# Feed-forward norms whose inverse root arrives behind the products, and a last expert turn without a gather

## The reference

```python
# first block, at its end
x = x + moe(rmsnorm(x, g_ffn), ...)               # top 4 of 32 experts, 3 x 1024x1024 weights each
gate = sigmoid(rmsnorm(x, g_ple) @ w_ple_gate)    # 1024x1024
x = x + (p @ w_ple_proj) * gate
x = rmsnorm(x, g_final)
# each of the two layers
x = x + 0.5 * swiglu(rms_norm(x, ffa_norm), ffa_w_in, ffa_w_out)   # 1024 -> 2 x 2816 -> 1024
h = rms_norm(x, mix_norm); ...                    # three mixers, gated and summed
x = x + (sum of gated branches) @ w_out
x = x + 0.5 * swiglu(rms_norm(x, ffb_norm), ffb_w_in, ffb_w_out)

def rms_norm(x, g): return x * rsqrt(mean(x * x, -1) + 1e-6) * g
def swiglu(h, w_in, w_out): gate, up = split(h @ w_in); return (silu(gate) * up) @ w_out
```

## Time and profile before

| | us |
|---|---|
| median of 3 runs | 2454.72 |
| lowest, highest | 2454.32, 2455.74 |
| profiled execution | 2455.39 |
| its span | 2453.6 |
| PE busy | 2419.6 |
| POOL busy | 1013.1 |
| DVE busy | 920.0 |
| ACT busy | 888.6 |

### The profile page before, as it was taken

One profiled execution on the slowest core, in us unless ns is written; L12 is line 12 of the kernel. 1 busy time (PEld: TensorE's weight loads), 2 busy tenths in 40 slices (PEclk: granted clock), 3 DMA queues, 4 the chain that ended last, 5 costly groups with the idle time before them and its releaser, 6 DMA issues.

```text
span 2453.6 us, 34874 instructions
## 1 busy us (share of the span) xinstructions
PE 2419.6 (99%) x13863; PEld 1713.7 (70%) x13863; DVE 920.0 (37%) x1736; ACT 888.6 (36%) x1457; POOL 1013.1 (41%) x430
## 2 busy tenths in 40 slices
PE   8999999999999999999999999999999999999999
PEld 6744444444444444468889899888888898998887
DVE  5622222222222222262248764332432388653322
ACT  6411111101111110154457624544444477425443
POOL 0000000000000000048877436788788785546886
PEclk9999999999999999999999999999999999999999
DMA  8799999999999999935555224465555553334654
GB/s 291 291 427 429 429 430 429 430 430 429 430 429 431 429 430 429 413 102 197 189 164 180 95 96 145 161 203 190 166 198 189 166 184 112 121 100 150 202 186 144
DMA packets 96584, 653.07 MB, mean 266 GB/s; under 512 B 10864, under 2 KB 13336, under 8 KB 69848
## 3 DMA queue, kind: packets, MB, share of 16 engines
q1 hardware_dynamic: 96472, 651.51, 69.1%
HBM read 650.22 MB, written 1.25 MB: 266 GB/s over the span
## 4 chain that ended last, share of the span: by engine, by line
PE 88%; DMA 8%; DVE 2%; ACT 1%; issue 1%; POOL 0%; SPq 0%; DVEq 0%; ACTq 0%
PE bank L2256 22%; PE bank L831 13%; PE bank L631 10%; PE bank L633 10%; PE bank L632 10%; PE bank L832 7%; DMA ring<-in_expert_units 4%; PE bank L2243 4%; DMA scratch<-in_expert_units 4%; PE bank L1226 3%; PE bank L2264 2%; PE bank L2272 1%; PE bank L1104 1%; PE bank L1075 1%; PE bank L1182 0%
## 5 line engine op out<-in xcount | busy, mean ns | idle before, releaser
L618 POOL TENSOR_TENSOR w_lo<-raw,w_hi 128x1024 fp32r<-128x1024 f32 (+2 forms) x424 | 1009.2, 2408 | 1198.2 <-ACT w_hi L612 1198.2
L2256 PE MATMUL bank<-ring,scratch 128*64 128x512 f32 x2304 | 513.4, 596 | 8.6 <-DMA ring<-in_expert_units 8.6
L831 PE MATMUL bank<-hT_both,w_hi 128*128 128x512 f32 x1408 | 498.3, 398 | 1.7 <-DVE hT_both L722 1.7
L612 ACT CAST w_hi<-raw 128x1024 fp32r<-128x1024 f32 (+2 forms) x424 | 422.3, 1042 | 169.1 <-PE bank L633 155.5
L832 PE MATMUL bank<-hT_both,w_lo 128*128 128x256 f32 x1408 | 395.9, 281 | 0.0
L2256 PEld LDWEIGHTS bank<-ring,scratch 128*64 128x64 f32 x2304 | 160.0, 137 | 323.2 <-issue 318.3
L831 PEld LDWEIGHTS bank<-hT_both,w_hi 128*128 128x128 f32 x1408 | 265.1, 188 | 67.6 <-issue 3.4
L2489 DVE TENSOR_TENSOR scratch<-bank,scratch 128x512 f32<-128x512 f32 x64 | 44.3, 692 | 594.8 <-PE bank L2272 590.7
L832 PEld LDWEIGHTS bank<-hT_both,w_lo 128*128 128x128 f32 x1408 | 266.7, 189 | 0.6
L909 DVE TENSOR_REDUCE scratch<-bank 128x256 f32<-128x512 f32 x88 | 60.8, 691 | 358.4 <-PE bank L832 358.4
L2256 PE MATMUL bank<-scratch 128*64 128x512 f32 x768 | 172.1, 596 | 2.2 <-DMA scratch<-in_expert_units 2.1
(11 more groups left out here) (372 smaller groups left out, 3360.1 us busy)
## 6 DMA issues: line engine op xcount, KB each, us to landing
ring<-in_expert_units SPq DMA_DIRECT2D x144, 2048.0 KB, 25.0
raw<-in_layer_halves SPq DMA_DIRECT2D x408, 512.0 KB, 4.4
scratch<-in_expert_units SPq DMA_DIRECT2D x47, 2048.0 KB, 25.9
ring<-in_first_units SPq DMA_DIRECT2D x11, 1024.0 KB, 10.0
ring<-in_ple_units SPq DMA_DIRECT2D x2, 2048.0 KB, 18.6
raw<-in_layer_halves SPq DMA_DIRECT2D x8, 424.0 KB, 3.4
scratch<-in_norm_gains SPq DMA_DIRECT2D x6, 512.0 KB, 6.1
raw<-in_layer_halves SPq DMA_DIRECT2D x4, 384.0 KB, 3.6
```

The lines of the kernel that those rows point to most:

```text
L612: k.nc.scalar.copy(k.w[0][i % SPLIT_SLOTS][:, at], k.raw[n % RAW_SLOTS][:, 0:at.stop - at.start]).then_inc(k.shared("weights_hi"), 1)
L618: k.nc.gpsimd.tensor_tensor(k.w[1][i % SPLIT_SLOTS][:, at], k.raw[n % RAW_SLOTS][:, 0:at.stop - at.start], k.w[0][i % SPLIT_SLOTS][:, at], ...
L831: nc.tensor.matmul(bank[:, :], w[0], both, start=start, stop=False)
L2256: last = nc.tensor.matmul(b[g * SL:(g + 1) * SL, :], lhsT[:, c, :], w[:, c, g, :], start=start and c == 0, stop=stop and c == 3)
```

## The change

Three parts.

1. **The root comes behind the products**, in all four norms ahead of a feed-forward block. DVE writes h = x * gain (`lnorm_gained`) as soon as a quarter of x is done, and PE transposes that. ACT and DVE compute the root meanwhile; DVE multiplies the unit matrix by it (`diag_dve`), PE multiplies ones by the two diagonals (`rstd_pe`), and the bank then holds the root of token s in column s of each partition. DVE copies it (128x256) and multiplies the gate sum and the up sum of each (u, j) by it: two more 128x256 products for each of the 22 column blocks of a block. The order of unit 0 is new (`ffn_first_pe`): half the columns of x first, so that the last quarter is turned behind 4 or 8 pairs, and the root's product stands before the last 8 pairs. The transposes move into the work ahead: into the last gate product, the last w_out product, the last feed-forward product. All spare products go, except four in layer 1's first norm. Squares are written to a scratch place instead of h.
2. **The fold with the final norm**: x is written back to SBUF before it is scaled, so projection banks come free earlier; the gained product and the final gain are two separate products; the final scaling is one 128x1024 step for each t, after the diagonals.
3. **The last turn**: the last group of four turns is written out behind the loop. In the last turn PE does no gather, only counts its semaphore up, and turns the selection before the transposes.

```diff
+def lnorm_gained(k, dve, n, t, half):
+    at = columns_half(half)
+    if t + half == 0:
+        dve.wait_ge(*k.at("gain_loaded", 16 * (n + 1)))
+    k.nc.vector.tensor_tensor(k.h[:, t, at], k.x[:, t, at], k.s(GAIN, D)[:, at], ALU.mult).then_inc(k.sem("h_ready"), 1)
+
+def diag_dve(k, dve, n, scales):
+    for t in range(NT):
+        dve.wait_ge(*k.at("norm_rstd", 4 * n + t + 1))
+        last = k.nc.vector.tensor_scalar(k.s(RSTD_DIAG, NT, P)[:, t, :], k.c("ident"), scales[t], None, ALU.mult)
+    last.then_inc(k.sem("diag_ready"), 1)
+
+def rstd_pe(k, pe, n):
+    b, full = k.claim(pe, ("rstd", n))
+    pe.wait_ge(*k.at("diag_ready", n + 1))
+    for t in range(NT):
+        last = k.nc.tensor.matmul(b[:, t * P:(t + 1) * P], k.c("ones"), k.s(RSTD_DIAG, NT, P)[:, t, :], start=(t == 0), stop=(t == NT - 1))
+    last.then_inc(full, 1)
...
+def late_norm_act(k, act, n, x_ready, between):
...
     square(0, 0)
     square(0, 1)
+    lnorm_hi(k, act, n, 0, 0)
+    lnorm_hi(k, act, n, 0, 1)
     lnorm_hi(k, act, n, 1, 0)
+    between()
+    if n == 2:
+        lnorm_hi(k, act, n, 1, 1)
+    square(1, 0)
+    square(1, 1)
+    if n == 0:
+        lnorm_hi(k, act, n, 1, 1)
+    lnorm_root(k, act, n, 0)
+    lnorm_root(k, act, n, 1)
+
+def late_norm_dve(k, dve, link, n, evacuate, x_written):
+    def gained(t, half):
+        evacuate(t, half)
+        x_written(t, half)
+        lnorm_gained(k, dve, n, t, half)
+    gained(0, 0)
+    gained(0, 1)
+    gained(1, 0)
+    lnorm_lo(k, dve, n, 0, 0)
+    lnorm_lo(k, dve, n, 1, 0)
+    gained(1, 1)
+    lnorm_lo(k, dve, n, 0, 1)
+    lnorm_lo(k, dve, n, 1, 1)
+    for t in range(NT):
+        lnorm_variance(k, dve, link, n, t)
+    diag_dve(k, dve, n // 2, [k.s(STATS, 8)[:, 2 * t:2 * t + 1] for t in range(NT)])
...
+def ffn_first_pe(k, pe, n):
...
+    if n == 0:
+        block(0, 0)
+        last_turned()
+        block(1, 0)
+        block(0, 1)
+    else:
+        block(0, 0, last_turned)
+        block(0, 1)
+        block(1, 0)
+    rstd_pe(k, pe, n)
+    block(1, 1)
...
 def ffn_dve(k, dve, link, n):
+    b, free = k.filled(dve, ("rstd", n))
+    V_.tensor_copy(rstd, b[:, 0:S]).then_inc(free, 1)
+    k.evacuated(dve, ("rstd", n))
...
-            both_added(k, silu[:, j, :], gate).then_inc(k.sem("gate_sum"), 1)
-            dve.wait_ge(*k.at("gate_sum", at))
+            link(both_added(k, silu[:, j, :], gate))
+            V_.tensor_tensor(silu[:, j, :], silu[:, j, :], rstd, ALU.mult).then_inc(k.sem("gate_sum"), 1)
             b, up_free = k.filled(dve, ("up", n, u, j))
             both_added(k, gate[:, 0:S], b).then_inc(up_free, 1)
             k.evacuated(dve, ("up", n, u, j))
+            link(V_.tensor_tensor(gate[:, 0:S], gate[:, 0:S], rstd, ALU.mult))
...
 def wout_pe
         for c in range(4):
+            if h == 1 and t + v == 2 and c in (0, 3):
+                (before_last if c == 0 else in_last)()
...
             pe.wait_ge(*k.at("sel_ready", it + 2))
+            if final:
+                turn_selection()
+                gather_next(0)
+                transposed(1, it)
+                gather_next(1)
...
 def ple_x_dve
     link(V_.tensor_tensor(b[:, :], b[:, :], sg, ALU.mult))
+    V_.tensor_tensor(x, b[:, :], x, ALU.add).then_inc(free, 1)
+    k.evacuated(dve, ("proj", v, t))
+    with k.inside(0):
+        V_.tensor_tensor(k.h[:, t, at], x, k.s(PLE_BOTH, D)[:, at], ALU.mult).then_inc(k.sem("h_ready"), 1)
+    V_.tensor_tensor(sg, x, k.s(PLE_GAINS, D)[:, at], ALU.mult).then_inc(k.sem("x_scaled"), 1)
...
 def layer_pe
     if k.part == 1:
-        warm_pe(k, pe, ("norm", 0, 0, 0), 8)
-    lnorm_pe(k, pe, 0, 0)
-    if k.part == 0:
-        spare_pe(k, pe)
-    else:
-        warm_pe(k, pe, ("norm", 0, 1, 0), 3)
-    lnorm_pe(k, pe, 0, 1)
-    if k.part == 1:
+        lnorm_pe(k, pe, 0, 1, (0,))
         warm_pe(k, pe, ("gate", 0, 0, 0), 4)
     ffn_pe(k, pe, 0)
...
-    wout_pe(k, pe)
-    lnorm_pe(k, pe, 2, 0)
-    warm_pe(k, pe, ("norm", 2, 1, 0), 9)
-    lnorm_pe(k, pe, 2, 1)
-    warm_pe(k, pe, ("gate", 1, 0, 0), 3)
-    ffn_pe(k, pe, 1)
+    wout_pe(k, pe, lambda: lnorm_pe(k, pe, 2, 0), lambda: lnorm_pe(k, pe, 2, 1, (0,)))
+    ffn_pe(k, pe, 1, next_norm)
```

More of the change, by code:

```diff
@@ L741, in warm_pe, with lnorm_pe @@
         k.nc.tensor.matmul(k.bank[b][:, :], act[:, 8, 0:P], act[:, 8:10, :], start=(j == 0), stop=(j == count - 1))
-def lnorm_pe(k, pe, n, t):
-    for half in range(2):
+def lnorm_pe(k, pe, n, t, halves=(0, 1)):
+    for half in halves:
         pe.wait_ge(*k.at("h_ready", 4 * n + 2 * t + half + 1))
@@ L860, in ffn_out_pe @@
             for v in range(2):
+                if t + v == 2 and before_last is not None:
+                    before_last()
                 for i in range(2):
@@ L2636, in ple_act @@
         ple_sigmoid_act(k, act, 0, v)
+    for v in range(2):
         ple_squares_act(k, act, 0, v)
-    with k.inside(0):
-        ple_root_act(k, act, 0)
     ple_sigmoid_act(k, act, 1, 0)
-    ple_squares_act(k, act, 1, 0)
-    ple_sigmoid_act(k, act, 1, 1)
-    nc.scalar.activation(st[:, 6:7], k.c("ones")[:, 0:1], ACT.Sqrt)
     with k.inside(0):
@@ L2680, in ple_variance_dve, with ple_final_dve @@
         V_.tensor_tensor(m, w, q, ALU.mult).then_inc(k.sem("variance_inverse"), 1)
[L2683 to L2700 removed]
+def ple_final_dve(k, dve, link, t):
+    dve.wait_ge(*k.at("last_ss", 2 * t + 2))
+    link(k.nc.vector.tensor_scalar(k.x[:, t, :], k.s(PLE_SG, NT, D)[:, t, :], ple_sums(k)[2][:, 2 * t:2 * t + 1], None, ALU.mult))
 def ple_dve(k, dve, link):
@@ L2736, in ple_dve @@
         lnorm_lo(k, dve, 0, 0, 1)
-    ple_variance_dve(k, dve, link, 1)
-    ple_h_dve(k, dve, 1)
+        lnorm_lo(k, dve, 0, 1, 0)
+    ple_x_dve(k, dve, link, 1, 1)
     with k.inside(0):
-        lnorm_lo(k, dve, 0, 1, 0)
         lnorm_lo(k, dve, 0, 1, 1)
-    ple_final_dve(k, dve, 1)
+    for t in range(NT):
+        ple_variance_dve(k, dve, link, t)
+    with k.inside(0):
+        diag_dve(k, dve, 0, [ple_sums(k)[2][:, 2 * t + 1:2 * t + 2] for t in range(NT)])
+    for t in range(NT):
+        ple_final_dve(k, dve, link, t)
 def layer_uses(start, first_banks):
@@ L3064, in layer_act @@
         splits.past(("wout", v, 0))
-    lnorm_act(k, act, 2, lambda t, v: k.evacuated(act, ("wout", t, v)))
-    for v in range(2):
-        splits.past(("wout", v, 1))
+    late_norm_act(k, act, 2, lambda t, v: k.evacuated(act, ("wout", t, v)), lambda: splits.past(("wout", 0, 1)))
+    splits.past(("wout", 1, 1))
     ffn_act(k, act, 1, splits)
@@ L3186, in _, with next_norm @@
         ple_gate_pe(k, pe, 1, 0)
+        with k.inside(0):
+            lnorm_pe(k, pe, 0, 0)
         ple_gate_pe(k, pe, 1, 1)
+        def next_norm():
+            with k.inside(k.part + 1):
+                lnorm_pe(k, pe, 0, 0)
         for layer in range(LAYERS):
             k.enter(layer)
-            layer_pe(k, pe)
+            layer_pe(k, pe, next_norm if layer + 1 < LAYERS else None)
     @block.scalar
@@ L3212, in from_layer, with x_written @@
                 ffn_out_dve(k, dve, 1, t, v)
-        for layer, x_pieces in enumerate((None, from_layer)):
+        def x_written(t, v):
+            with k.inside(0):
+                k.evacuated(dve, ("ffn_out", 1, t, v))
+        for layer, x_pieces in enumerate((None, (from_layer, x_written))):
             k.enter(layer)
```

261 lines of the change are left out of this document (129 added, 132 removed).

## The result

The changed kernel takes 2465.68 us (median of 6 runs, 2462.88 to 2468.07) against 2455.61 for the kernel before, timed beside it (6 runs): a ratio of 1.0044, 95% interval 1.0033 to 1.0054. The forecast was 2452.5, the range ended at 2458.5, and slower had the smallest chance. The profiled execution took 2466.69 us with a span of 2464.9, 11.3 more than the span of before.

The account below looks back on a forecast made before the run. PE was taken as the bound, busy 99% of the span. Last turn -1.85, layer 0's first block +0.1, layer 1's +1.9 and second blocks -2.4 sum to -2.25 us: median 2452.5, 8-in-10 range 2446.5 to 2458.5.

Parts of the forecast that it names:

- x times the norm's vector: Ahead of the feed-forward blocks: DVE's 128x512 product in SBUF priced at 0.65 us, from 0.6 to 0.7.
- like L930's 0.42: New 128x256 root products and root copy on DVE: priced like an existing 0.42 us row, 0.46 with a link.
- Last turn: Last expert turn: dropping PE's unused gathers saves 1.85 us, bounds -4.1 and 0, limited by the last unit's transfer.
- Layer 0's first block: Ahead of that block: unit 1 starts 1.6 us earlier, a slow clock stretch costs 1.7; +0.1 in all.
- two final scalings: DVE ahead of unit 1 in layer 0's first block: 128x1024 steps at 0.86 us each at most, lower bound 0.43.
- L3081 and the tables: Layer 0's first block: a one-column DVE step and 16 rope table products stay, unmoved, before the feed-forward's first sum.
- Second blocks: Ahead of both layers' second feed-forward blocks: PE waits 1.5 us, unit 1 starts 1.2 us earlier; -1.2 each, -2.4.
- rival (a): All four places: new bank 0 waits bring further slow clock stretches, +1.2 or +4.6 us in all; chance 0.19.
- Layer 1's first block: Ahead of that block: unit 1 starts 0.2 us later and a new slow clock stretch costs 1.7; +1.9.
- Rival (c): First blocks: L3081's 1.39 and 2.02 us may be a wait, up to 3.4 us less, 2449.1 to 2447.4; chance 0.16.
- (b): Ahead of the blocks: unit 1 is not held by DVE's tables and new products, saving 20.4 us, 2434.4; chance 0.05.
- (d): Last expert turn: its part does nothing or its copied code must be fetched, 2454.4 to 2457.4; chance 0.10.

## Why the prediction was wrong

**The step that failed is a price**: "x times the norm's vector, 128x512 in SBUF, is 0.6 to 0.7; I take 0.65", and the new products "like L930's 0.42", "with a link 0.46, bounds 0.3 and 0.7". L930 and every row behind these prices either read a bank or fell into a pause of POOL. In the changed kernel the same shapes in SBUF took 1.53 and 1.74 us in the mean. The forecast held no term for DVE waiting for POOL. Where PE waits ahead of unit 1, and that DVE's low part ends the wait, was right at all four places; in layer 1 what lay behind it was not the tables, as forecast, but the late root product.

- Last turn: -1.85 forecast, -1.7 measured from the landing on. Right. The timing alone does not tell the step from nothing.
- Layer 0's first block: +0.1 forecast, +2.25 measured. Unit 1 starts 0.85 us later than forecast (1086.76, against 1086.5 less the 0.59 by which P came early). The two final scalings cost 2.0 more than forecast. L3081 and the tables, which the forecast moved unchanged, 5.4 us with two holds in them, took 4.0 with one: 1.4 less. That part of the small error is luck. The clock took 2.9 instead of 1.7, 1.2 more.
- Second blocks: -1.2 forecast, +1.22 and +1.33 measured. Two of four products with the vector were held, 2.11 and 2.73 us instead of 0.65: 3.5 us, of which 2.5 reached unit 1. No slow clock there (1.00), so 1.3 us of waiting beside transposes did not bring rival (a). With the operands in banks the two blocks measured -0.38 and -1.12, nearly the forecast.
- Layer 1's first block: +1.9 forecast, +6.08 measured. Held: 2.44 and 2.12 for the vector, 2.39 for the first gate product, 5.2 us over the prices; unit 1 starts 4.5 later than forecast, the slower products ahead of the block among it. Unit 0 began 5.1 us later than forecast (1770.69 less 3.19, against 1762.4), no earlier than in the kernel before. The tables, carried over at 6.1 us with two holds, took 2.0 and were no longer in the way. The clock behind unit 1's start cost 1.4 (forecast 1.7).
- Mixers: nothing forecast, +0.31 and +0.70 measured. Layer 0's lies where ScalarE waits 0.76 us for a transfer of weights (at 1329.40). Layer 1's is a wait of PE for h, 0.73 us at 1961.96, behind a variance step of one column that a late piece of POOL's held, 0.81 us for 0.16.
- The rest is the last unit's landing, +1.06, by chance of that execution: over the twelve profiles it lands between 1021.1 and 1024.6.

Rival (c) had the clue in hand. It said of L3081's 1.39 and 2.02 us for one column that it might be a wait, and that no other single column took so long. It was one, but for POOL, and I asked only what would be saved if it went, not which of the new instructions would be held in the same way. The row of 2.02 us stood in the earlier trace rows; POOL's timeline of the same microseconds was not laid beside it. The trace of before also had the price itself, in the mixers, where one SBUF product of 128x512 takes 0.68 us twice and 2.85 twice (min/median/max in ns):
```profile
L1373 DVE TENSOR_TENSOR h_rows<-const,scratch x4: 676/1761/2851, 1370.8 to 2064.1; 128x512 f32<-128x512 f32 x4
```

Rival (a) named the right side, with the wrong mechanism: one slow stretch more at layer 0's block (1.4 us) and one more at layer 1's (some 1.2), both behind waits that the held instructions made or lengthened. (b) and (d) did not come about.

## What to carry to other kernels

Before an instruction is priced on VectorE, ask where its operands are and what GpSimd does at that time: rows of the same shape and another memory are no price, and a single instruction whose duration has no relation to its size is a hold whose partner must be found. On a path that others wait for, one operand in a bank was worth more than the copy that it cost (12 copies more, 9 us less). Serial work of an engine in front of the first thing that frees a bank belongs behind it, even if that work itself becomes no cheaper.

## What the runs showed of the hardware that was not expected

- An SBUF product on VectorE that begins during a piece of GpSimd's subtraction waits for the rest of that piece: 64 columns took 1.60 us and one column 2.19, against 0.23 and 0.15 with GpSimd idle, and 512 columns up to 2.7 (0.69 free). It ends a fixed time behind the piece, 0.28 us for 256 columns, 0.55 for 512, 1.08 for 1024.
- A product with a number, one SBUF tensor, is held too (2.27 us, 0.18 free). Reductions and products that read a bank are not (0.69 to 0.70, 0.42 to 0.43 in both cases).
- GpSimd can be the one that waits: its pair at 1777.75 took 5.86 us instead of 4.8. Eight table products of 64 columns ran on VectorE from 1777.86 for 1.16 us, at 0.21 each, not held, and the first piece took 3.52 us instead of 2.4.
- The clock fell to its lower level behind 2.10 us of waiting in layer 1, and did not behind 1.64 and 1.32 in layer 0's second block. Spare products in the wait kept it at 1.00 in layer 0, and the kernel was no faster.
